# Row normalisation by diagonal matrices in a hybrid decoder block

## The reference

```
x = x + 1/2 * SwiGLU(RMSNorm(x))                       first FFN, 1024 -> 2 * 2816 -> 1024
h = RMSNorm(x); u, v, gates = split(h @ W_in)          mixer, 1024 -> 5120
x = x + (sig(g_A) * S5(u) + sig(g_B) * Conv(v)) @ W_out
x = x + 1/2 * SwiGLU(RMSNorm(x))                       second FFN
out = RMSNorm(x)

RMSNorm(x) = x * rsqrt(mean(x * x, features) + 1e-6) * gain
```

## Time and profile before

| | us |
|---|---|
| median of 3 runs | 2176.78 |
| lowest and highest | 2176.57, 2177.51 |
| the profiled execution's own time | 2176.12 |
| its span, from the first to the last instruction | 2174.0 |

### The profile page before, as it was taken

One profiled execution on the slowest core, in us unless ns is written; L12 is line 12 of the kernel. 1 busy time (PEld: TensorE's weight loads), 2 busy tenths in 40 slices (PEclk: granted clock), 3 DMA queues, 4 the chain that ended last, 5 costly groups with the idle time before them and its releaser, 6 DMA issues.

```text
span 2174.0 us, 31669 instructions
## 1 busy us (share of the span) xinstructions
PE 2137.9 (98%) x10191; PEld 1768.0 (81%) x10191; DVE 1702.5 (78%) x2163; ACT 946.3 (44%) x1560; POOL 665.4 (31%) x749
## 2 busy tenths in 40 slices
PE   7999999999999999999999999999999999999998
PEld 6788888888878888888888788887888888888886
DVE  5877877879995999999999659767687767665557
ACT  6455555544455122222224224135465555544444
POOL 2886645969990000000000430500024442000000
PEclk9999999999999999999999999999999999999999
DMA  5335876488774344544435642895256764337754
GB/s 171 80 121 166 273 228 212 145 293 295 250 264 149 102 145 151 153 138 151 153 117 172 209 141 79 305 322 191 68 180 207 230 213 159 101 113 265 232 194 174
DMA packets 316194, 397.43 MB, mean 183 GB/s; under 512 B 28625, under 2 KB 201265, under 8 KB 315984
## 3 DMA queue, kind: packets, MB, share of 16 engines
q1 hardware_dynamic: 293264, 315.71, 45.1%
q0 software_dynamic: 21104, 76.24, 10.5%
q10 hardware_dynamic: 1744, 4.46, 0.5%
HBM read 266.81 MB, written 129.52 MB: 182 GB/s over the span
## 4 chain that ended last, share of the span: by engine, by line
PE 91%; DVE 6%; ACT 2%; issue 1%; DMA 1%; SPq 0%; ACTq 0%; DVEq 0%
PE PU L1502 11%; PE PU L1504 11%; PE PU L1503 11%; PE PU L1442 9%; PE PU L1444 9%; PE PU L1443 9%; PE PD L1377 4%; PE PD L1379 4%; PE PD L1378 4%; PE PU L1377 3%; PE PU L1379 3%; PE PU L1378 3%; PE PD L1578 1%; PE PD L1579 1%; PE PD L1580 1%
## 5 line engine op out<-in xcount | busy, mean ns | idle before, releaser
L1442 PE MATMUL PU<-Hhi,Whi 128*128 128x512 f32 x896 | 352.2, 393 | 0.8 <-issue 0.7
L1444 PE MATMUL PU<-Hhi,Wlo 128*128 128x512 f32 x896 | 348.9, 389 | 0.0
L1443 PE MATMUL PU<-Hlo,Whi 128*128 128x512 f32 x896 | 348.8, 389 | 0.0
L2608 DVE SCALAR_TENSOR_TENSOR XT<-XT,wq 128x1024 f32<-128x1024 f32 x240 | 312.9, 1304 | 8.2
L1442 PEld LDWEIGHTS PU<-Hhi,Whi 128*128 128x128 f32 x896 | 168.2, 188 | 38.5 <-issue 4.3
L1444 PEld LDWEIGHTS PU<-Hhi,Wlo 128*128 128x128 f32 x896 | 168.2, 188 | 35.2
L1443 PEld LDWEIGHTS PU<-Hlo,Whi 128*128 128x128 f32 x896 | 168.3, 188 | 34.9 <-issue 0.7
L1502 PE MATMUL PU<-Hhi,Dhi 128*128 128x512 f32 x480 | 186.9, 389 | 0.0
L1503 PE MATMUL PU<-Hlo,Dhi 128*128 128x512 f32 x480 | 186.8, 389 | 0.0
L1504 PE MATMUL PU<-Hhi,Dlo 128*128 128x512 f32 x480 | 186.8, 389 | 0.0
L1377 PE MATMUL PD<-Dhi,Ahi 128*128 128x512 f32 x416 | 162.8, 391 | 4.7 <-DVE Alo L2182 4.3
(11 more groups left out here) (414 smaller groups left out, 5081.0 us busy)
## 6 DMA issues: line engine op xcount, KB each, us to landing
TAB<-in_w_ffn_down POOLq DMA_DIRECT2D x44, 512.0 KB, 5.0
d_sb<-TAB POOLq DMA_DIRECT2D x44, 512.0 KB, 3.8
Wraw<-in_w_ffn_up SPq DMA_DIRECT2D x80, 256.0 KB, 4.1
XT<-in_w_ffn_up SPq DMA_DIRECT2D x80, 256.0 KB, 5.0
d_sa<-XT SPq DMA_DIRECT2D x80, 256.0 KB, 2.4
Wraw<-in_w_in SPq DMA_DIRECT2D x32, 512.0 KB, 5.2
d_act<-G SPq DMA_DIRECT2D x48, 256.0 KB, 2.5
WRd<-d_sb SPq DMA_DIRECT2D x44, 256.0 KB, 4.1
```

The lines of the kernel that those rows point to most:

```text
L1442: mm(o_, Whi[s][:, side, k, :], Hhi[:, k, hs[h]], start=k == 0, stop=False)
L1443: mm(o_, Whi[s][:, side, k, :], Hlo[:, k, hs[h]], start=False, stop=False)
L1444: last = mm(o_, Wlo[s][:, side, k, :], Hhi[:, k, hs[h]], start=False, stop=k == KT - 1)
L2608: stt(CVb, z_, w_, CVb, ALU.mult, ALU.add).then_inc(m["conv"], 1)
```

## The change

Rows aren't scaled any more. VectorE multiplies the identity by the row factors of each of the four row blocks (`diagonals`), into the buffer G[1]; the turn then is a plain float32 matmul of the raw row block, stationary, by that diagonal matrix, moving, in place of the transpose of a scaled row block. `x_scale`, `scaled`, `scaled_rows`, `mix_scaled`, `Hrow` and their calls on ScalarE and VectorE go. In the first half of nmx the diagonals stand at step (6,2) of VectorE's queue; elsewhere they follow the row factors in `row_scale`. Since G[1] is in use, one of four buffers for the output projection's activations moves to `rt`. The reciprocal root has 9 steps in place of 11 or 12: the seed, one round of third order with two constants (`rows_cube`) and one Newton round; the squares come scaled by 1/1024 from ScalarE, so that epsilon and half sums are added in one step. The same 9 steps stand in the layer norm and the final norm.

```diff
+ROW_SCALE = 1.0 / math.sqrt(D)
+CUBE_A, CUBE_B, CUBE_C = -10.0 / 3.0, 5.0, 3.0 / 8.0
...
-    Hrow = over("Hhi", 0, "Hrow", [P, KT, L])
...
-            return at4(sf, i) if i < 2 else G[i - 2][:, :]
+            return at4(sf, i) if i < 2 else G[0][:, :] if i == 2 else at4(rt, 1)
...
+    dg = lambda j: G[1][:, j * P:(j + 1) * P]
...
-    FIN_STEPS = 12
+    FIN_STEPS = 9
-    RS_STEPS = {"nf1": 11, "nmx": 12, "nf2": 12}
+    RS_STEPS = {"nf1": 9, "nmx": 9, "nf2": 9}
...
                 for j in range(4):
-                    last = tr(banks[k % 4][:, j * P:(j + 1) * P], xn_block(name, h, j, k), ident[:, :])
+                    last = mm(banks[k % 4][:, j * P:(j + 1) * P], XT[:, 4 * h + j, k * P:(k + 1) * P], dg(j), start=True, stop=True)
                 last.then_inc(norm["tr"], 1)
...
-            fn(af[:, 0:D], XT[:, j, :], ACT.Square, accum_out=tok[:, 0, j:j + 1]).then_inc(norm["sq"], 1)
+            fn(af[:, 0:D], XT[:, j, :], ACT.Square, scale=ROW_SCALE, accum_out=tok[:, 0, j:j + 1]).then_inc(norm["sq"], 1)
...
-            for j in (4 * h,):
-                fn(XT[:, j, :], XT[:, j, :], ACT.Copy, scale=tok[:, 1, j:j + 1]).then_inc(norm["xn"], 1)
...
             split_step(OUTP, 6, 1)
-            act.wait_ge(*norm_at("nf2", "rs", RS_STEPS["nf2"]))
-            scaled_rows("nf2", OUTP, 0, (0, 1))
             split_step(OUTP, 6, 2)
-            scaled_rows("nf2", OUTP, 0, (2, 3))
-            act.wait_ge(x_st, 16 * (J + 4))
             split_step(OUTP, 6, 3)
...
         quadrant(FFN1, 1, 1, 6, 12)
-        scaled("nmx", FFN1, 1)
...
         out_proj()
-        scaled("nf2", OUTP, 1)
...
             if halves:
-                dve.wait_ge(chain.sem, chain.up(tt(ss, ss, s2, ALU.add)))
-            dve.wait_ge(chain.sem, chain.up(ts(nv, ss, 1.0 / D, RMS_EPS, ALU.mult, ALU.add)))
+                dve.wait_ge(chain.sem, chain.up(stt(nv, ss, RMS_EPS, s2, ALU.add, ALU.add)))
+            else:
+                dve.wait_ge(chain.sem, chain.up(ts(nv, ss, RMS_EPS, None, ALU.add)))
             dve.wait_ge(chain.sem, chain.up(ts(r.bitcast(I32), nv.bitcast(I32), -0.5, RSQRT_SEED, ALU.mult, ALU.add)))
+        def rows_cube(chain, cols_):
...
+            dve.wait_ge(chain.sem, chain.up(tt(nt, r, r, ALU.mult)))
+            dve.wait_ge(chain.sem, chain.up(tt(nt, nt, nv, ALU.mult)))
+            dve.wait_ge(chain.sem, chain.up(stt(nt, nt, CUBE_A, nt, ALU.add, ALU.mult)))
+            dve.wait_ge(chain.sem, chain.up(stt(r, nt, CUBE_B, r, ALU.add, ALU.mult)))
...
         def rows_rsqrt(chain, cols_, halves):
             rows_start(chain, cols_, halves)
-            for _ in range(3):
-                rows_round(chain, cols_)
+            rows_cube(chain, cols_)
+            rows_round(chain, cols_)
...
+        def diagonals(name, h):
+            if h:
+                dve.wait_ge(*norm_at(name, "tr", KT))
+            elif name == "nmx":
+                dve.wait_ge(act_saved[1], SAVED0[FFN2][1])
+            elif name == "nf2":
+                dve.wait_ge(ma_saved[1], 16 * KT)
+            for j in range(4):
+                ts(dg(j), ident[:, :], tok[:, 1, 4 * h + j:4 * h + j + 1], None, ALU.mult).then_inc(norm["xn"], 1)
...
         def row_scale(name, h):
             dve.wait_ge(*norm_at(name, "sq", 4 * (h + 1) if name == "nf1" else 8 * (h + 1)))
             rows_rsqrt(norm_chain, slice(4 * h, 4 * h + 4), name != "nf1")
+            diagonals(name, h)
...
-        def x_scale(h):
-            for j in (4 * h + 1, 4 * h + 2, 4 * h + 3):
-                ts(XT[:, j, :], XT[:, j, :], tok[:, 1, j:j + 1], None, ALU.mult).then_inc(norm["xn"], 1)
...
-        down(FFN1, {(0, 5): lambda: sum_low(FFN1, NSP - 1, SAVED0[FFN1]), (3, 9): lambda: split_pair(R_MIX, 0), (5, 9): mix_rows_start, (5, 10): mix_rows_round,
-                    (6, 0): mix_rows_round, (6, 1): mix_rows_round,
-                    (6, 9): lambda: turned("nmx", 0, 0), (6, 10): lambda: turned("nmx", 0, 1)})
+        down(FFN1, {(0, 5): lambda: sum_low(FFN1, NSP - 1, SAVED0[FFN1]), (3, 9): lambda: split_pair(R_MIX, 0), (5, 9): mix_rows_start, (5, 10): mix_rows_cube,
+                    (6, 0): mix_rows_round,
+                    (6, 2): lambda: diagonals("nmx", 0), (6, 9): lambda: turned("nmx", 0, 0), (6, 10): lambda: turned("nmx", 0, 1)})
```

More of the change, by code:

```diff
@@ L73 @@
 D_GOES_ON = (3, 4, 5)
-XN_IN_H = (("nf2", 0),)
 D_ROWS = ((0, 1), (1, 0), (0, 0), (1, 1))
@@ L411, in wo_stored @@
         return wo_st[t % 2][i], base + 16 * (t // 2 + 1)
-    NORM_BASE = {"nf1": dict(sq=0, rs=0, xn=0, tr=0, hi=0, lo=0), "nmx": dict(sq=8, rs=22, xn=8, tr=16, hi=16, lo=16),
-                 "nf2": dict(sq=24, rs=46, xn=16, tr=32, hi=32, lo=32)}
+    NORM_BASE = {"nf1": dict(sq=0, rs=0, xn=0, tr=0, hi=0, lo=0), "nmx": dict(sq=8, rs=18, xn=8, tr=16, hi=16, lo=16),
+                 "nf2": dict(sq=24, rs=36, xn=16, tr=32, hi=32, lo=32)}
     def norm_at(name, key, value):
         return norm[key], NORM_BASE[name][key] + value
-    FIN_STEPS = 12
+    FIN_STEPS = 9
     ROT = 6 + 2 * PR + 6
@@ L1671, in turned @@
                     .then_inc(norm["hi"], 1)
-        def x_scale(h):
-            act.wait_ge(*norm_at("nf1", "rs", RS_STEPS["nf1"] * (h + 1)))
-            for j in (4 * h,):
-                fn(XT[:, j, :], XT[:, j, :], ACT.Copy, scale=tok[:, 1, j:j + 1]).then_inc(norm["xn"], 1)
[L1679 to L1698, removed]
         def quadrant(S, h, dh, p, done, js=range(4)):
@@ L1708, in quadrant @@
                 n = 4 * h + j
-                fn(junk[S], xo(S, h, j)[:, hs[dh]], ACT.Square, accum_out=tok[:, 4 * dh, n:n + 1]).then_inc(sq, 1)
+                fn(junk[S], xo(S, h, j)[:, hs[dh]], ACT.Square, scale=ROW_SCALE, accum_out=tok[:, 4 * dh, n:n + 1]).then_inc(sq, 1)
                 if S is not FFN2 and (h, dh) == (0, 0):
@@ L1948, in _ @@
         split_pair(0, 1, False)
-        x_scale(0)
         act.wait_ge(gain_tr, 1)
@@ L1956, in _ @@
         split_pair(1, 0, False)
-        x_scale(1)
         act.wait_ge(row_ld, 16 * 10)
@@ L1963, in _ @@
                     (5, 6): lambda: quadrant(FFN1, 0, 0, 4, 4, (0,)), (5, 7): lambda: quadrant(FFN1, 0, 0, 4, 4, (1,)),
-                    (5, 8): lambda: quadrant(FFN1, 0, 0, 4, 4, (2,)), (5, 9): lambda: quadrant(FFN1, 0, 0, 4, 4, (3,)), (6, 2): mix_scaled, (6, 3): lambda: scaled_rows("nmx", FFN1, 0, (2, 3)),
+                    (5, 8): lambda: quadrant(FFN1, 0, 0, 4, 4, (2,)), (5, 9): lambda: quadrant(FFN1, 0, 0, 4, 4, (3,)),
                     (6, 6): lambda: quadrant(FFN1, 1, 0, 5, 8), (6, 9): lambda: turned("nmx", 0, 0),
@@ L2197, in rsqrt @@
             step(ts(dst.bitcast(I32), NV.bitcast(I32), -0.5, RSQRT_SEED, ALU.mult, ALU.add))
-            for _ in range(3):
-                step(stt(NT, dst, -0.5, dst, ALU.mult, ALU.mult))
-                step(tt(NT, NT, NV, ALU.mult))
-                step(stt(dst, NT, 1.5, dst, ALU.add, ALU.mult))
+            step(tt(NT, dst, dst, ALU.mult))
+            step(tt(NT, NT, NV, ALU.mult))
+            step(stt(NT, NT, CUBE_A, NT, ALU.add, ALU.mult))
+            step(stt(dst, NT, CUBE_B, dst, ALU.add, ALU.mult))
+            step(stt(NT, dst, -0.5 * CUBE_C ** 3, dst, ALU.mult, ALU.mult))
+            step(tt(NT, NT, NV, ALU.mult))
+            step(stt(dst, NT, 1.5 * CUBE_C, dst, ALU.add, ALU.mult))
         def turned(name, h, kq):
@@ L2215, in rows_start @@
             if halves:
-                dve.wait_ge(chain.sem, chain.up(tt(ss, ss, s2, ALU.add)))
-            dve.wait_ge(chain.sem, chain.up(ts(nv, ss, 1.0 / D, RMS_EPS, ALU.mult, ALU.add)))
+                dve.wait_ge(chain.sem, chain.up(stt(nv, ss, RMS_EPS, s2, ALU.add, ALU.add)))
+            else:
+                dve.wait_ge(chain.sem, chain.up(ts(nv, ss, RMS_EPS, None, ALU.add)))
             dve.wait_ge(chain.sem, chain.up(ts(r.bitcast(I32), nv.bitcast(I32), -0.5, RSQRT_SEED, ALU.mult, ALU.add)))
+        def rows_cube(chain, cols_):
+            ss, r, nv, nt, s2 = [tok[:, i, cols_] for i in range(5)]
+            dve.wait_ge(chain.sem, chain.up(tt(nt, r, r, ALU.mult)))
+            dve.wait_ge(chain.sem, chain.up(tt(nt, nt, nv, ALU.mult)))
+            dve.wait_ge(chain.sem, chain.up(stt(nt, nt, CUBE_A, nt, ALU.add, ALU.mult)))
+            dve.wait_ge(chain.sem, chain.up(stt(r, nt, CUBE_B, r, ALU.add, ALU.mult)))
         def rows_round(chain, cols_):
             ss, r, nv, nt, s2 = [tok[:, i, cols_] for i in range(5)]
-            dve.wait_ge(chain.sem, chain.up(stt(nt, r, -0.5, r, ALU.mult, ALU.mult)))
+            dve.wait_ge(chain.sem, chain.up(stt(nt, r, -0.5 * CUBE_C ** 3, r, ALU.mult, ALU.mult)))
             dve.wait_ge(chain.sem, chain.up(tt(nt, nt, nv, ALU.mult)))
-            dve.wait_ge(chain.sem, chain.up(stt(r, nt, 1.5, r, ALU.add, ALU.mult)))
+            dve.wait_ge(chain.sem, chain.up(stt(r, nt, 1.5 * CUBE_C, r, ALU.add, ALU.mult)))
         def rows_rsqrt(chain, cols_, halves):
             rows_start(chain, cols_, halves)
-            for _ in range(3):
```

(7 more changed lines are left out.)

## The result

The changed kernel takes 2190.56 us (median of 4 runs, 2189.47 to 2190.96), the kernel before 2177.15 us on the same chip (4 runs, 2176.57 to 2177.61). The ratio is 1.0058, with a 95% interval from 1.0046 to 1.007: slower, by 13.4 us. The forecast was 2193.0 with a range from 2188.5 to 2199.0. The profiled execution has a span of 2188.0 us against 2174.0, so the traces have 14.0 us to explain.

What follows compares the result with a forecast made beforehand. TensorE, busy 2137.9 of 2174.0 us, was taken to bound the kernel. Dearer turns (+20.1) and the other terms summed to +16.3 us; on the profiled 2176.12, plus 0.7 for the median, this gave 2193.0 us, range 2188.5 to 2199.

Steps and rivals of the forecast that it cites:

- ten turns at full pace: TensorE's turns other than the first two: each 3.76 us in place of 1.75, +20.1 us (17.4 to 22.5).
- start: First two turns: TensorE starts at 12.65 us, runs at half pace for 3.5 us, ends at 22.0; +0.9 us.
- first norm, second half: TensorE's 0.6 us wait for the last scaled row goes, by a shorter chain and quicker diagonals; -0.6 us.
- mixer's norm, first half: Inside the down projection: 0.99 us wait stays, diagonals add 0.8 or 0.9, other waits lose 0.6; +0.3 us.
- mixer's norm, second half: Diagonals are ready before TensorE comes, so its 1.4 us wait for ScalarE's four scaled rows goes; -1.4 us.
- third norm: Output projection's last part: two waits, 2.6 us together, go and one split comes 0.16 later; -2.4 us.
- end: After TensorE's last matmul the final chain of 12 steps loses 3 steps of 0.198 us; -0.6 us.
- Two passes: In the turns, each float32 multiply makes two records where a transpose makes one: 384 in place of 192.
- rival (a): In the turns, a multiply costs what a transpose does, 0.109 us a block: -7.9 us, 2168.9, faster; chance 0.04.
- The price of a pass: In the turns, each record of a multiply takes 0.1175 us, 0.235 a block, as read from L1545.
- Rival (b): In the turns, a block costs four transposes, 0.437 us: +55.1 us, 2231.9; chance 0.03.
- Rival (c): In the turns, the weight load isn't hidden, 0.192 us a record, 0.384 a block: +44.9 us, 2221.7; chance 0.02.

Runs made afterwards that it cites:

- e2: Changed kernel, diagonals and their waits kept, each multiply by a diagonal replaced by a transpose of the raw block against the identity; 2168.48 us, ratio 0.9958.
- e3: Changed kernel with each block's multiply issued twice into the same place; 2234.30 us, ratio 1.026.
- e6: e4 with 80 transposes of the identity, results never read, added on TensorE ahead of the first turn; 2170.40 us, ratio 0.9964.
- e8: Changed kernel with 72 transposes of the identity, results never read, added on TensorE ahead of the first turn; 2187.85 us, ratio 1.0051.
- e1: Kernel before with the nine-step reciprocal root alone, rows scaled and transposed as before; 2175.21 us, ratio 0.9989.
- e4: Kernel before with the nine-step root, scaled rows and transposes kept, the scaling reordered or shared to remove three waits; 2169.79 us, ratio 0.9966.
- e5: e4 with the mixer's root one to two slots later in the down projection and ScalarE's scaled rows one slot later; 2171.17 us, ratio 0.9972.

## Why the prediction was right

The terms of the forecast and what the traces show (after - before, us):

| term | forecast | measured |
|---|---|---|
| ten turns at full pace | +20.1 | +18.2 |
| start | +0.9 | +0.3 |
| first norm, second half | -0.6 | -0.8 |
| mixer's norm, first half | +0.3 | +0.1 |
| mixer's norm, second half | -1.4 | -1.9 |
| third norm | -2.4 | -3.4 |
| end | -0.6 | -0.6 |
| not forecast | 0 | +2.1 |
| sum | +16.3 | +14.0 |

The sum came out 2.3 too high, and closer than its terms: they were too high by 4.4 together, and 2.1 us that no term held made up for nearly half of it. That part is luck.

**Two passes.** Right, and it is the whole of the case: 384 records, all of the loss gone in e2, doubled in e3. The row of L1545, the same operation elsewhere in the kernel, told this ahead; rival (a), one pass, and with it "faster", stood on the columns alone. **The price of a pass** is the term that was mis-sized: 0.1175, taken from sixteen records of L1545, is 0.112 in the turns, between the value taken and the lower bound of 0.109. Ten turns come to 1.82 more each and not 2.01. The single starts of L1545 in the trace of before are 0.112 apart as well, and only the last is followed by 0.205 to the next line; the forecast spread this gap over the sixteen as if it were price. **Rival (b)**, four times a transpose by the rule of the transpose mode in "TensorE: Matmul & The Clock Gate" of the Trainium skill, Terms: the measured ratio is 2.0 (0.223 to 0.109). The same two rows can be put beside the kernel's float32r matmuls, 512 columns every 0.23 us, so about 0.057 for 128: the multiply costs 3.9 times that, the transpose 1.9 times. "FP8 and Floating Point Precision" of the Trainium skill, TensorE Precision Notes, says that a true FP32 multiply makes four passes; the trace agrees if one counts by the float32r pass. **Rival (c)**, the weight load: at a median of 0.192 us each it stays hidden, since records come every 0.112.

**The start.** Right in kind: half pace from the start of the work, not until a fixed time. But the 3.5 us were misread. In the trace of before the second sixteen took 2.27 us to the next matmul, where sixteen at full pace take 1.67, so that part of these came slowly too: single starts are 0.22 apart until 20.1, 4.7 us from the first. In the changed kernel the slow pace lasted 3.1 us, near the 3.5 assumed; with the 4.7 us of before the forecast's own sum gives +1.5 in place of +0.9, so that this misreading helped. The term came out 0.6 too high by the price of a block (0.3) and by the 0.494 taken for a block at half pace (0.3), for which e3 shows 0.43. The diagonals took 0.2 each from start to start, as forecast. e6 and e8 show that the half pace goes with the first work. How long it lasts, from the first start to the last slow one, differs from trace to trace (2.8 us in e2 to 5.8 in e1 and e6); there is one trace of each kernel, so whether this goes with the kernel or with the execution stays open.

**The mixer's first half.** The sum was near, the places weren't, and that is luck. The 0.99 didn't stay as it was: one wait of 1.50 stands at the change of banks, with three instructions of VectorE on 4 columns at 1.19, 1.28 and 1.38 us around it, and the waits after it went. Behind the diagonals at (6,2), which start from 647.4 to 648.1 us, TensorE waits nothing until 660 us and once 0.16 after it: neither the 0.8 or 0.9 us of wait forecast there nor the upper bound (GpSimd stretching them to 1.15 each) came. VectorE and GpSimd of the changed kernel:

```profile
647.40 1.00 DVE L2224 TENSOR_SCALAR G<-ident,tok 128x128 f32<-128x128 f32 x4
...
647.16 0.40 POOL L1225 TENSOR_TENSOR TAB<-TAB,TMP 128x128 f32<-128x128 f32 x1
647.63 0.49 POOL L1226 TENSOR_TENSOR Bsc<-TAB,TMP 128x128 f32<-128x128 f32 x1
```

GpSimd is at work there, but at instructions of 0.4 to 0.5 us, not of the 1.3 to 1.8 us beside which single small instructions of VectorE took over 1 us. Three diagonals took 0.27 us and one 0.42; at the start they took 0.28 or 0.29. e1 and e4 have the same 1.5 with no diagonals at all, so it doesn't come from the diagonals but goes with the root's new pieces (e5, which moves them, is without it).

**The removed waits** came out as read, each somewhat more than its row, and e4 had them too by moving the rows. At the third norm the difference falls from 10.0 (at 1508 us of before) to 6.5, 3.4 us: the 2.6 of the earlier trace rows, 0.4 at the first turn for a gather, and the rest in shorter steps; the forecast had left 0.16 and the 0.4 standing. **Not forecast** are 0.6 us between 46 and 573 us, 0.7 between 700 and 1508 (0.4 of it in one wait of L1434, 0.9 for 0.5), 0.3 between 1560 and the last gather, and 0.5 behind the last scaling. Their causes stay open; e6 gives back as much in the first of these stretches when its start is earlier (TensorE waits more for VectorE there), so that part of an earlier or later start doesn't reach the end. That this is what the 0.6 are is argued, not shown.

## What to carry to other kernels

Look for the new operation in the old trace before asking for its price: the count of records (two for each float32 matmul) settled the sign here, and only a price per record, taken from start to start with the gap behind the group kept apart, settles the size. When a kernel's bound engine is busy 98% of the span, an edit that moves work from idle engines onto it has to be paid by waits that it removes; list those waits first and ask whether a shorter chain and another order remove them, as they did here (2169.79 in place of 2190.56). A wait that is moved off one place, as in e5, can come back at the next: look at what else the edit moves.

## What the runs showed of the hardware

- A float32 matmul of 128 x 128 by 128 columns is two records that start 0.112 us apart, 0.223 in all (changed kernel, e3), and a transpose of a 128 x 128 float32 block is one record of 0.109 (before, e2). The weight load of the multiply takes 192 ns, that of the transpose 141 ns (median, e2), and both lie under the matmuls.
- TensorE ran its first records of steady work at 0.21 to 0.22 us in place of 0.11. This lasted 2.8 us in e2, 3.1 in the changed kernel (some 15 records), 4.7 in the kernel before, 4.9 in e3 and 5.8 in e6, where 80 transposes took 11.6 us to the next start and 80 x 0.109 is 8.7. The granted clock in those stretches reads 1.00 (2.4 GHz) all the same.
- Beside a GpSimd instruction of 1.3 to 1.8 us, single VectorE instructions of 4 columns took 1.07 to 1.39 us in place of 0.16, and ended with it (e4: 631.46 and 631.45); they were TENSOR_TENSOR and SCALAR_TENSOR_TENSOR as well as the TENSOR_SCALAR of the earlier trace rows. Beside GpSimd instructions of 0.4 to 0.5 us, TENSOR_SCALARs of 128 x 128 took 0.27 to 0.42.
